# One decoder step on one core: a new order for the index scores, taps and sums in turns, rank matmuls in twos, a weight in the eviction

## What is computed

```python
z = jnp.einsum('btd,de->bte', _rms_norm(x, norm_g), w_in)
q = _rms_norm(zq.reshape(B, T, N_HEADS, HEAD_DIM), q_g)     # q_g: one weight per column of a head
k = _rms_norm(zk.reshape(B, T, N_KV_HEADS, HEAD_DIM), k_g)
u = glu_a * jax.nn.sigmoid(glu_b)
...
s = jnp.einsum('thd,ld->thl', qi, ki) * (IDX_DIM ** -0.5)   # index scores, 8 heads of 64
score = jnp.einsum('th,thl->tl', wi * (N_IDX_HEADS ** -0.5), jax.nn.relu(s))
_, idx = lax.top_k(jnp.where(k_pos <= q_pos, score, -jnp.inf), 256)
...
bias = rel_bias[_rel_bucket(q_pos - idx)]                   # one value per head
p = softmax(q . k[idx] * HEAD_DIM ** -0.5 + bias)           # attention over the 256 keys
...
conv = depthwise conv of u over 31 rows, LayerNorm, silu    # "taps"
y = x + concat(attn * silu(gate_a), conv * silu(gate_c)) @ w_out
```

## Time and profile before

| | before |
|---|---|
| median of 3 runs | 1022.67 us (1020.48 to 1022.98) |
| the profiled execution | 1022.88 us, its span 1021.0 us |
| TensorE busy | 918.9 us, 90% of the span |
| VectorE busy | 690.4 us, 68% |
| ScalarE busy | 348.6 us, 34% |
| granted TensorE clock, mean | 0.947 of full |

### The profile page before, as it was taken

One profiled execution on the slowest core, in us unless ns is written; L12 is line 12 of the kernel. 1 busy time (PEld: TensorE's weight loads), 2 busy tenths in 40 slices (PEclk: granted clock), 3 DMA queues, 4 the chain that ended last, 5 costly groups with the idle time before them and its releaser, 6 DMA issues.

```text
span 1021.0 us, 11394 instructions
## 1 busy us (share of the span) xinstructions
PE 918.9 (90%) x3952; PEld 508.5 (50%) x3952; DVE 690.4 (68%) x1532; ACT 348.6 (34%) x750; POOL 84.4 (8%) x89
## 2 busy tenths in 40 slices
PE   3999999999988679999969898797697889999998
PEld 2866666664332236666534244453465555445432
DVE  4218999998587788888898888956587564332101
ACT  6311101101344568888600000313855363321000
POOL 0120112001133000000000000001011010310000
PEclk9899999999999979999989799798799799999999
DMA  8272011213255050020030000005021111321111
GB/s 298 92 206 27 1 47 39 84 47 119 83 167 168 16 177 30 1 83 1 0 103 32 11 31 1 1 1 214 21 64 52 32 35 39 124 83 41 64 63 43
DMA packets 35459, 69.90 MB, mean 68 GB/s; under 512 B 9625, under 2 KB 12097, under 8 KB 35393
## 3 DMA queue, kind: packets, MB, share of 16 engines
q1 hardware_dynamic: 28233, 43.99, 13.3%
q0 software_dynamic: 7168, 25.17, 7.6%
HBM read 58.52 MB, written 11.11 MB: 68 GB/s over the span
## 4 chain that ended last, share of the span: by engine, by line
PE 78%; DVE 13%; ACT 3%; issue 3%; DMA 1%; SPq 1%; DVEq 0%; POOL 0%; ACTq 0%; POOLq 0%
PE ps L529 74%; PE ps L532 5%; DVE SC L1392 2%; DVE ct L1314 1%; DMA xn<-in_x_prompt 1%; DVE pv L1570 1%; ACT PTs L1018 1%; DVE eqm L1420 1%; ACT uT L1191 1%; DVE LB L1571 1%; DVE uT L1776 0%; ACT relu L1122 0%; ACT sqj L1031 0%; DVE junk L1420 0%; DVE zN L1594 0%
## 5 line engine op out<-in xcount | busy, mean ns | idle before, releaser
L529 PE MATMUL ps<-xT,W 128*128 128x344 f32 x960 | 286.9, 457 | 0.0
L529 PEld LDWEIGHTS ps<-xT,W 128*128 128x128 f32 x960 | 180.9, 191 | 90.8 <-issue 3.5
L529 PE MATMUL ps<-W,xT 128*128 128x512 f32 (+3 forms) x576 | 224.8, 546 | 0.0
L1340 DVE SCALAR_TENSOR_TENSOR ctmp<-uT,chw,ctmp 128x1024 f32<-128x1024 f32 x116 | 153.0, 1319 | 4.0
L529 PEld LDWEIGHTS ps<-W,xT 128*128 128x128 f32 (+1 forms) x576 | 95.8, 188 | 114.4 <-issue 113.8
L1159 ACT ACTIVATE sgj<-SC,cand,sense 128x1024 bf16<-128x1024 f32 (+2 forms) x96 | 104.4, 1088 | 25.8 <-DVE cand L1474 20.8
L1018 ACT ACTIVATE PTs<-ps 128x512 f32<-128x512 f32 (+3 forms) x96 | 43.0, 483 | 128.2 <-PE ps L532 123.5
L1807 DVE TENSOR_TENSOR ps<-ps,TP 128x256 f32<-128x256 f32 (+1 forms) x64 | 26.4, 412 | 69.4 <-PE ps L529 69.0
L1204 ACT ACTIVATE nsq<-ps 128x512 f32<-128x512 f32 (+1 forms) x18 | 10.7, 596 | 163.2 <-DVE nss L1583 115.8
L532 PE MATMUL ps<-Cc,Pm 128*128 128x128 f32 x288 | 47.3, 304 | 17.6 <-ACT PTs L1018 17.0
L529 PE MATMUL ps<-W,uT 128*128 128x512 f32 x128 | 60.1, 613 | 0.0
(11 more groups left out here) (309 smaller groups left out, 1007.6 us busy)
## 6 DMA issues: line engine op xcount, KB each, us to landing
W<-in_w_in SPq DMA_DIRECT2D x8, 2048.0 KB, 8.9
xn<-in_x_prompt SPq DMA_DIRECT2D x8, 512.0 KB, 7.7
W<-in_w_out SPq DMA_DIRECT2D x1, 4096.0 KB, 13.7
resid<-in_x_prompt SPq DMA_DIRECT2D x16, 256.0 KB
out<-resid SPq DMA_DIRECT2D x16, 256.0 KB
out<-V SPq DMA_DIRECT2D x8, 256.0 KB
out<-zN SPq DMA_DIRECT2D x8, 256.0 KB, 2.0
bias_rows<-tprow SPq DMA_DIRECT2D x1, 1536.0 KB
```

Source lines behind the costliest of these rows:

```text
L529: return nc.tensor.matmul(out, lhsT, rhs, start=start, stop=stop)
L1340: ins = vec.scalar_tensor_tensor(conv[:, c, :] if j == CW - 1 else acc_, src, chw[:, c, j:j + 1], acc_, ALU.mult, ALU.add)
```

## The change

The index stage is ordered anew: five v tiles run first, then two chunks, then six turns, each a `cached` with six chunks; a v tile opens at every second turn and that turn stands between its halves. From row block 4 on the sums of a block's two pieces alternate, and a sum waits for the last sum into the same piece only. Taps alternate between two groups of channels from the twentieth on. `sc16b` moves out of `SC`. Two k tiles leave the search's units (`K_EARLY`) and run behind them. Rank matmuls are issued in pairs, both banks taken first; the first pair of a tile stands in the middle of its `natural`. q's tiles are transposed without the weight, which a scale operand per partition (`qgc`, loaded by two small transfers) brings in at the eviction. `key_bias` runs one head per tile from the ninth tile on, with buffers of its own (`kbt`, `ohb` and `rbB` elsewhere). ScalarE's loops follow the same order.

```diff
-    sc16 = [sb("sc16a", [16, 32, 2, 16], F32, rKV), sb("sc16b", [16, 32, 2, 16], F32, rSC + 12800)]
+    sc16 = [sb("sc16a", [16, 32, 2, 16], F32, rKV), sb("sc16b", [16, 32, 2, 16], F32, rGC)]
...
+    V_AHEAD = 5
+    def sums_order():
+        order, n = [], 0
+        while n < len(CHUNKS):
+            two = CHUNKS[n][0] >= 4
+            order += [(n, 0), (n + 1, 0), (n, 1), (n + 1, 1)] if two else [(n, 0), (n, 1)]
+            n += 2 if two else 1
+        return order
+    SUMS = sums_order()
+    TURN_AT = {2 + 6 * j: 2 + j for j in range(6)}
+    TURN_BEFORE = {6 * j: 2 + j for j in range(6)}
...
+    ALONE = 19
+    def tap_order():
+        order, at_ = [(0, j) for j in range(ALONE)], [ALONE, 0, 0, 0]
+        for c in range(3):
+            while at_[c] < CW:
+                order += [(c, at_[c]), (c + 1, at_[c + 1])]
+                at_[c] += 1
+                at_[c + 1] += 1
+        return order + [(3, j) for j in range(at_[3], CW)]
+    TAPS = tap_order()
...
-    K_EARLY = 4
+    K_EARLY = 2
...
+        for t in range(V_AHEAD):
+            natural("v", t, 2)
+            if t == 0:
                 own_score()
+            if t == 1:
+                cached(0)
+            if t == V_AHEAD - 2:
+                cached(1)
+        def turn_chunks(j):
+            cached(2 + j)
+            for n in range(2 + 6 * j, min(8 + 6 * j, len(CHUNKS))):
                 index_scores(n)
+        for n in range(2):
+            index_scores(n)
+        for j in range(0, 6, 2):
+            natural("v", V_AHEAD + j // 2, 2, lambda: turn_chunks(j))
+            turn_chunks(j + 1)
+        for n in range(38, len(CHUNKS)):
+            index_scores(n)
...
-        def rank_row(s):
+        def rank_rows(one, two):
-            b, tl = RANKED[s]
-            r = 32 * (b // 2)
-            o = begin(("gr", s), f"b{6 + s % 2}")
-            mm(o[:, :], OH[r:r + 32, b % 2, tl * P:(tl + 1) * P], dM[r:r + 32, 0:SEG]).then_inc(plan.fill_sem(("gr", s)), 1)
+            for s in (one, two):
+                begin(("gr", s), f"b{6 + s % 2}")
+            for s in (one, two):
+                b, tl = RANKED[s]
+                r = 32 * (b // 2)
+                mm(pt(("gr", s)), OH[r:r + 32, b % 2, tl * P:(tl + 1) * P], dM[r:r + 32, 0:SEG]).then_inc(plan.fill_sem(("gr", s)), 1)
...
-            wait(zn_ready, n + 1)
+            if g == "k":
+                wait(zn_ready, n + 1)
+            else:
+                wait(*plan.drained(("z", g, t)))
...
         for n, (g, t) in enumerate(NORMED):
+            s0 = 4 * (n - 5)
             if n >= K_EARLY:
-                natural(g, t)
+                natural(g, t, between=(lambda: rank_rows(s0, s0 + 1)) if 5 <= n <= 8 else None)
...
             if 5 <= n <= 8:
-                for s in range(4 * (n - 5), 4 * (n - 4)):
-                    rank_row(s)
+                rank_rows(s0 + 2, s0 + 3)
...
-                    act.wait_ge(made["key_bias"], 1)
+                if g == "q":
+                    act.wait_ge(q_weight, 1)
-                     scale=1.0 if g == "k" else -HD ** -0.5)
+                     scale=1.0 if g == "k" else qgc[:, 0:1])
...
+        v.wait_ge(q_weight_in, 32)
+        vec.tensor_scalar(qgc[:], qgc[:], -HD ** -0.5, None, ALU.mult).then_inc(q_weight, 1)
...
-                c, j = DVE_CHUNKS[m // CW], m % CW
+                c, j = TAPS[m]
+                    if c >= 2:
+                        v.wait_ge(taps_done, TAPS.index((c - 2, CW - 1)) + 1)
-                acc_ = ctmp[:, m // CW % 2, :]
+                acc_ = ctmp[:, c % 2, :]
-                    v.wait_ge(taps_done, m)
+                    v.wait_ge(taps_done, TAPS.index((c, j - 1)) + 1)
...
+        def weighted(u):
+            n, e = SUMS[u]
             i, hp, a = CHUNKS[n]
+            h = 2 * hp + e
+            src, dst = relu[:, u % 4, 0:width(n)], sc(i)[:, a:a + width(n)]
+            v.wait_ge(*plan.drained(("ix", n, e)))
+            if h == 0:
+                vec.tensor_scalar(dst, src, wI[:, i, 0:1], None, ALU.mult).then_inc(relu_used, 1)
+                return
+            for w in range(u):
+                if CHUNKS[SUMS[w][0]][0::2] == (i, a):
+                    last = w
+            v.wait_ge(relu_used, last + 1)
+            vec.scalar_tensor_tensor(dst, src, wI[:, i, h:h + 1], dst, ALU.mult, ALU.add).then_inc(relu_used, 1)
+        for n in range(len(CHUNKS)):
+            if n in TURN_BEFORE:
+                cached_turn(TURN_BEFORE[n])
+            if n % 2 == 0:
+                for u in range(2 * n, 2 * n + 4):
+                    weighted(u)
...
-            link(vec.tensor_tensor(pv3[:], ohb[:], rbB[:, :, h].unsqueeze(1).broadcast_to([P, 16, NBK]), ALU.mult))
-            last = vec.reduce_sum(LB[:].rearrange("p t b h -> p (t b) h")[:, :, h], pv3[:], AXX)
+            link(vec.tensor_tensor(kbt[:], ohb[:], rbB[:, :, h].unsqueeze(1).broadcast_to([P, 16, NBK]), ALU.mult))
+            last = vec.reduce_sum(LB[:].rearrange("p t b h -> p (t b) h")[:, :, h], kbt[:], AXX)
...
+            if g == "q" and t < NT:
+                return
...
-            if n == 8:
-                for h in range(H):
-                    key_bias(h)
+            if n >= 8 and n - 8 < H:
+                key_bias(n - 8)
...
+        for half in range(2):
+            sp.dma_start(qgc[64 * half:64 * half + 64, :], qg[0:1, :].rearrange("a d -> d a"), allow_slow_non_contiguous=True).then_inc(q_weight_in, 16)
```

More of the change, by code:

```diff
@@ L272, in build @@
     zq = sb("zq", [NB, 512], F32, rSD)
+    ohb = sb("ohb", [P, 16, NBK], F32, rSD)
+    kbt = sb("kbt", [P, 16, NBK], F32, rQZ)
     NC = offs["selnew"][0]
@@ L365, in build @@
     zn_ready = sem("zn_ready")
+    q_weight = sem("q_weight")
+    q_weight_in = sem("q_weight_in")
     zn_out = [sem(f"zn_out{i}") for i in range(2)]
@@ L444, in width @@
         return min(512, (i + 1) * P - a)
-    FIRST_SLOT, SLOTS = 5, NT + 1
-    CACHED_AT = {1: (0,), 4: (1,), 5: (2, 3), 6: (4, 5), 7: (6, 7)}
-    def chunks_in(s):
-        last = sum(1 for x in CHUNKS if x[0] < NT - 1)
-        if s == SLOTS - 1:
-            return range(last, len(CHUNKS))
-        k, n = s - FIRST_SLOT, SLOTS - 1 - FIRST_SLOT
-        return range(max(k, 0) * last // n, max(k + 1, 0) * last // n)
-    def cached_in(s):
-        return CACHED_AT.get(s, ())
-    def halves(s):
-        c = chunks_in(s)
-        return c[:len(c) // 2], c[len(c) // 2:]
+    V_AHEAD = 5
[9 more added lines that the diff above has]
+    TURN_BEFORE = {6 * j: 2 + j for j in range(6)}
     EVACUATED_EARLY = NT
@@ L713, in index_scores @@
                 mm(pt(("ix", n, e))[:, 0:width(n)], qiT[r, hp, i * P:(i + 1) * P], kiT[r, a:a + width(n)]).then_inc(plan.fill_sem(("ix", n, e)), 1)
-        for s in range(SLOTS):
-            one, two = halves(s)
-            def between():
-                for n in one:
-                    index_scores(n)
-            if s < NT:
-                natural("v", s, 2, between)
-            else:
-                between()
-            if s == 0:
-                own_score()
-            for n in cached_in(s)[:1]:
-                cached(n)
-            for n in two:
-                index_scores(n)
-            for n in cached_in(s)[1:]:
-                cached(n)
+        for t in range(V_AHEAD):
+            natural("v", t, 2)
+            if t == 0:
+                own_score()
+            if t == 1:
[5 more added lines that the diff above has]
+            for n in range(2 + 6 * j, min(8 + 6 * j, len(CHUNKS))):
+                index_scores(n)
+        for n in range(2):
[5 more added lines that the diff above has]
+            index_scores(n)
         for g, m in STAGE_UNITS:
@@ L907, in query_rows @@
                 b = r // 2
-                wait(zn_ready, len(NORMED))
+                wait(zn_ready, NT + 2)
                 o = begin(("qb", b), "b7")
@@ L1112, in cached_out, with index_relu @@
                 scores_out(7)
-        def index_relu(n):
-            for e in range(2):
+        def index_relu(lo, hi):
+            for u in range(lo, hi):
+                n, e = SUMS[u]
                 tag = ("ix", n, e)
-                u = 2 * n + e
                 act.wait_ge(*plan.full(tag))
@@ L1138, in evacuate @@
                 a, n = piece_rows(m)
+                if m == 0:
+                    act.wait_ge(scd_out[1], 128)
                 piece_out(g, m, gcT[:, m // 3, a:a + n], sT[:, 3], ACT.Silu)
-        for s in range(SLOTS):
-            one, two = halves(s)
-            for n in one:
-                index_relu(n)
-            if s < NT:
-                evacuate("v", s)
-            for n in cached_in(s)[:1]:
-                cached_out(n)
-            for n in two:
-                index_relu(n)
-            for n in cached_in(s)[1:]:
-                cached_out(n)
+        for t in range(V_AHEAD):
+            evacuate("v", t)
+            if t == 1:
+                cached_out(0)
+            if t == V_AHEAD - 2:
+                cached_out(1)
```

(10 more changed lines are left out.)

37 lines of the change are left out of this document (9 added, 28 removed).

## The result

| | before | after |
|---|---|---|
| median (4 runs each) | 1021.82 us (1020.48 to 1022.98) | 1003.66 us (1001.72 to 1006.15) |
| ratio, 95% interval | | 0.9825 (0.980 to 0.985) |
| profiled execution, its span | 1022.88, 1021.0 us | 1001.72, 999.9 us |
| TensorE, VectorE busy | 918.9, 690.4 us | 908.3, 672.3 us |

The time lies in the stated range, 985 to 1009, which takes in the better case and the second rival, and 2.7 us outside the forecast's own range, 988 to 1001. The chain answers the earlier trace rows: TensorE has a little more of it.

The account below looks back on a forecast made before the run. TensorE was taken to bound the kernel (78% of the chain, VectorE 13%). Terms -16 - 12.2 + 11 + 2 - 12.5 = -27.7 took 1022.9 to 995 us; own range 988 to 1001, stated range 985 to 1009.

Parts of the forecast that it names:

- better case: Index-stage waits less than worked out (-5), clock staying up at the second variance (-2), ranks (-2): 986 us, 10%.
- second rival: Threshold search not limited by TensorE but by the ScalarE and VectorE loop, so nothing gained there: 1007 us, 12%.
- Index stream: Index-score stage up to the first search count: earlier first sum, cheaper sums, DMA wait gone, search begins at 347.5: -16 us.
- first rival: Index stage: the step of the weighted sums doesn't fall and stays at 0.85 us: 1004 us, 16%.
- Search: Threshold search: two k tiles fewer in TensorE's stream shorten 31 rounds by 0.39 us each: -12.2 us.
- Hand-over: End of search to "eqoff": the two moved k tiles stand ahead of the prefix sum VectorE waits for: +11 us.
- Ranks: Rank matmuls issued in twos: each second pair costs two matmuls' time in waits: +2 us, ends 0 and +4.
- Tiles: Normalised tiles: key bias one head per tile, q's weight in the eviction, TensorE's wait goes: -12.5 us.
- Taps, loads of the weight: Before the index stage: taps in twos and two small loads of q's weight, both covered by other waits: costed at nothing.
- other side's rival: TensorE's granted clock falls in the index stretch, to 0.6, making the kernel slower: 1027 us, 4%.

Follow-up runs that it names:

- e2: Changed kernel with ScalarE's relus back in chunk order, VectorE's sums still alternating: 1001.9 us, ratio 0.981.
- e10: Changed kernel with relus in chunk order and, in each index-stage turn, two chunks run before the cached scores: 996.7 us, ratio 0.974.
- e1: Changed kernel with the index stage's sums and relus in the old order, a chunk's two heads side by side: 1003.7 us, ratio 0.983.
- e4: Changed kernel with four k tiles in the search again instead of two: 1004.6 us, ratio 0.985.
- e6: Changed kernel with the rank matmuls issued one by one behind the tile's transposes, not in pairs: 1001.2 us, ratio 0.981.
- e12: Changed kernel with the 124 taps in the old order, one group of channels after the other: 1005.1 us, ratio 0.988.

## Why the prediction was nearly right

*Index stream, -16: wrong, the step is the wait term.* Everything ahead of it held. The first sum came at 265.95 (predicted 265.8). Sums in stock step by 0.66 (0.67), the DMA wait is gone, and VectorE's own work in the stage, its 90.6 less the waits, is 71.2 us (70.9: transposes 23.1, sums 47.0 and the 0.8 at the seam). But I had 10.8 us of waits in the stage, and it has 19.4 (24.0 less the 4.6 ahead of the first sum). Two of them:

```profile
273.76 2.78 DVE L1424 SCALAR_TENSOR_TENSOR SC<-relu,wI,SC 128x384 f32<-128x384 f32 x4 [5.23 <-ACT relu L1144]
...
343.12 0.49 DVE L1418 TENSOR_SCALAR SC<-relu,wI 128x512 f32<-128x512 f32 x1 [3.83 <-ACT relu L1144]
```

Ahead of chunk 2 it is 5.2 where I had 5.1, and behind the eighth turn 3.8 for 2.7; behind the four turns between them it is 6.8 for 3.0, and in and between the groups of four sums, where I had put nothing, 3.5. I had looked at each sum's wait and at the turns from VectorE's side alone, taking it that TensorE would be ahead wherever it had the time. I didn't read the order of the relus on ScalarE, which the change turned with the sums, against the banks that TensorE asks for: in block 7 that is the 3.22 us for four sums, and e2 wins 2.8 us back. And behind a turn I had counted 3.2 us to the next relu's sum, without ScalarE's evictions of the cached scores, where it is 4.0 and the order could have spared it (e10: 4.3).

*The first rival gave the right number for a wrong reason.* It said 1004 if the sums kept their 0.85. They didn't; the loop over the banks and the turns cost what they had saved. A time that matches is no proof of its mechanism: e1 undid half of the step and lost nothing. The rule that it was built on falls here: e2's fourteen sums at 0.66 against 0.85, and the taps at 1.20 against 1.38, show that what an operation waits for does set its step. The same section of the Trainium skill ("VectorE: DVE Perf Modes", "The DRAIN you can't avoid") also says that a next operation that isn't held starts earlier. That half of it agrees with the runs: a sum that needn't wait for the one before starts 0.66 us behind its start, and a sum is busy for 0.75.

*Search, -12.2: right,* 13.3. Two successive rounds begin at

```profile
405.49 0.75 DVE L1447 TENSOR_SCALAR_CACHE_REDUCE eqm<-SD,cand 128x513 bf16<-128x513 f32 x1
...
409.40 0.75 DVE L1447 TENSOR_SCALAR_CACHE_REDUCE eqm<-SD,cand 128x513 bf16<-128x513 f32 x1
```

3.91 apart, the floor that I had read from one round; 24 of the 31 take 3.91 or 3.92, and their mean fell from 4.42 to 4.00 (predicted 4.37 to 3.98), so the second rival falls; e4 gives the search's 12.3 back. VectorE now waits less than 0.1 us for the group sum in most rounds, so fewer columns should bring no more; that was not run.

*Hand-over, +11: right in kind, 2.3 too high.* I had scaled from nine matmuls at 9.67 us, which ran at a lower clock; here 24 took 20.85 at the full one. In e6, at the same place of the same program, they took 23.44 and the wait was 11.45, so both sizes occur (e10 has the longer one too).

*Ranks, +2: right* (1.5, and e6 gives 2.2 back). *Tiles, -12.5: right, 2 too high:* the 9.1 us went, but the tile behind the first variance runs slower too in this execution. Before it took 7.11 at 658.55; in the changed kernel both such tiles read like this one:

```profile
633.24 3.63 PE L543 MATMUL ps<-Cc,lnsq 128*128 128x1 f32 x32
636.73 8.81 PE L543 MATMUL ps<-W,xT 128*128 128x512 f32 x16
```

I had named the second of these as a possible gain, not the first as a possible loss. But that is not the change's doing: in e1, e4, e6 and e10, where the tiles' code is the changed kernel's, one of the two keeps its 7.11 (the stage takes 90.9 to 92.5 there), and by the 1.7 us of one such tile the term would be about -12, my estimate. *Taps, loads of the weight: right at nothing* (e12 for the taps; the loads were not tried alone). The other side's rival fell: the clock in the index stage is 1.00.

## What to carry to other kernels

A loop over buffers has as many orders as it has engines: when the consumer's order is turned, read the producer's release of each bank in that order too, or keep the producer's order and turn only the consumer's (e2). Where the engine behind stands still at a turn, put work that needs nothing from the turn ahead of what does, two chunks were enough here (e10). And a time that hits a forecast says nothing about its terms: undo the term, and read from the trace whether the edit undid all of it (e1 undid half).
